# Dense stage of a hybrid decoder layer: places, orders and stores around its two ends

## The reference

```python
h = rms(x);  proj = h @ w_in                       # q | k | v | B | C | xc
a = diff_attention(...);  c = short_conv(...)
x = x + concat(a, c) @ w_out
x = x + peer(rms(x))
# peer: per token and head (8 heads) the 16 best of 128*128 experts, by two lists of 128 keys
act = gelu(einsum("tkd,td->tk", u[experts], h)) * gates
y   = einsum("tk,tkd->td", act, v[experts])        # 128 experts per token
```

## Time and profile before

| | us |
|---|---|
| median of 3 runs | 2944.31 |
| the profiled execution | 2943.42 |
| its span, first to last instruction | 2941.6 |
| TensorE busy | 2884.6 |
| VectorE busy | 2374.1 |
| ScalarE busy | 1054.5 |
| GpSimd busy | 1589.7 |

### The profile page before, as it was taken

One profiled execution on the slowest core, in us unless ns is written; L12 is line 12 of the kernel. 1 busy time (PEld: TensorE's weight loads), 2 busy tenths in 40 slices (PEclk: granted clock), 3 DMA queues, 4 the chain that ended last, 5 costly groups with the idle time before them and its releaser, 6 DMA issues.

```text
span 2941.6 us, 40454 instructions
## 1 busy us (share of the span) xinstructions
PE 2884.6 (98%) x14881; PEld 2557.2 (87%) x14881; DVE 2374.1 (81%) x3078; ACT 1054.5 (36%) x1375; POOL 1589.7 (54%) x1022
## 2 busy tenths in 40 slices
PE   8999999999999999999999999999999999999998
PEld 6888778878899999999999999999997888778777
DVE  6555788755679888988889898899777999889988
ACT  4121433341333333434333343344233333334333
POOL 1000444400115765666656566577867888877852
PEclk9999999999999999999999999999999999999999
DMA  8997887778868999999999899999999999999998
GB/s 296 332 356 271 284 275 262 248 283 312 302 235 311 325 349 316 333 326 341 319 323 340 301 338 330 335 338 368 330 360 395 408 419 416 418 420 420 421 417 359
DMA packets 327440, 995.33 MB, mean 338 GB/s; under 512 B 64565, under 2 KB 181313, under 8 KB 241793
## 3 DMA queue, kind: packets, MB, share of 16 engines
q1 hardware_dynamic: 179056, 515.94, 47.1%
q0 software_dynamic: 110656, 447.10, 42.1%
q10 hardware_dynamic: 37584, 30.43, 3.2%
HBM read 873.67 MB, written 119.67 MB: 338 GB/s over the span
## 4 chain that ended last, share of the span: by engine, by line
PE 69%; DVE 12%; DMA 7%; issue 5%; POOL 5%; ACT 1%; ACTq 0%; DVEq 0%; SPq 0%; POOLq 0%
PE ps L1979 21%; PE ps L1981 21%; PE ps L1980 21%; DMA v_ring<-in_peer_v,experts 4%; DVE x_rows L1829 3%; PE ps L2220 3%; POOL dots L946 3%; POOL v_ring L957 2%; DVE u_row L1820 2%; DMA v_two<-in_peer_v 1%; DVE uT_lo L1788 1%; DVE x_one L1927 1%; DVE uT_lo L1793 1%; DVE v_lo L1878 1%; DMA u_row<-in_peer_u,experts 1%
## 5 line engine op out<-in xcount | busy, mean ns | idle before, releaser
L1979 PE MATMUL ps<-hT_hi,uT_hi 128*128 128x384 f32 x2048 | 698.2, 341 | 8.1 <-DVE uT_lo L1788 4.6
L1981 PE MATMUL ps<-h2T_lo,uT_hi 128*128 128x384 f32 x2048 | 686.0, 335 | 0.0
L1980 PE MATMUL ps<-hT_hi,uT_lo 128*128 128x384 f32 x2048 | 684.9, 334 | 0.0
L938 POOL DMA_INDIRECT grid<-gates,grid_cells x256 | 518.6, 2026 | 105.3 <-issue 78.0
L1979 PE MATMUL ps<-v_hi,a_hi 128*128 128x512 f32 x1024 | 406.8, 397 | 23.5 <-DVE v_lo L1878 22.8
L1980 PE MATMUL ps<-v_hi,a_lo 128*128 128x512 f32 x1024 | 404.7, 395 | 0.0
L1981 PE MATMUL ps<-v_lo,a_hi 128*128 128x512 f32 x1024 | 404.6, 395 | 0.0
L1303 ACT ACTIVATE v_hi<-v_two 128x2048 fp32r<-128x2048 f32 x126 | 241.7, 1919 | 450.9 <-PE ps L1981 385.5
L1979 PEld LDWEIGHTS ps<-hT_hi,uT_hi 128*128 128x128 f32 x2048 | 384.7, 188 | 17.6 <-DVE uT_lo L1788 8.1
L1980 PEld LDWEIGHTS ps<-hT_hi,uT_lo 128*128 128x128 f32 x2048 | 385.0, 188 | 1.9
L1981 PEld LDWEIGHTS ps<-h2T_lo,uT_hi 128*128 128x128 f32 x2048 | 384.4, 188 | 0.0
(11 more groups left out here) (210 smaller groups left out, 4933.8 us busy)
## 6 DMA issues: line engine op xcount, KB each, us to landing
v_two<-in_peer_v SPq DMA_DIRECT2D x63, 2048.0 KB, 11.5
u_tile<-in_peer_u SPq DMA_DIRECT2D x65, 1024.0 KB
u_tile<-uT_all SPq DMA_DIRECT2D x63, 1024.0 KB
grid_rows<-grid SPq DMA_DIRECT2D x32, 1024.0 KB, 15.3
near_rows<-in_peer_u SPq DMA_DIRECT2D x25, 1024.0 KB, 8.7
uT_all<-near_turned SPq DMA_DIRECT2D x100, 256.0 KB, 7.0
w_raw<-in_w_in SPq DMA_DIRECT2D x24, 1024.0 KB, 9.1
wc_raw<-in_w_in SPq DMA_DIRECT2D x48, 512.0 KB, 6.0
```

The costliest lines, as they stand in the source:

```text
L938: pool.indirect_dma_start(out=grid, out_offset=bass.IndirectOffsetOnAxis(ap=grid_cells[:, d, col:col + 1], axis=0), in_=gates[:, 2 + d, co ...
L1979: mm(out, a_hi, b_hi, start=first, stop=False)
L1980: mm(out, a_lo, b_hi, start=False, stop=False)
L1981: return mm(out, a_hi, b_lo, start=False, stop=last)
```

## The change

What it does:

- A new place `v_four` (where a row buffer of u, u_row0, was) takes tile 4, and `v_one` is used a second time, for tile 5. Each is loaded by a DMA of 1 MiB. grid_rows1 moves by 8 KB and the pair buffers a_hi, a_lo change places to make room. v_two[0] is first used for tiles 8 and 9.
- SyncE's order at the front: tile 4, the second group, tile 5, then the third group, tiles 6 and 7, x_one, and on as before. The second group's load no longer waits for the last dots.
- ScalarE splits tile 1 right behind the gelu of the last sweep tile, ahead of the two stores of its products.
- VectorE: `add(126)` comes after tile 1's remainder and the last dot; `weigh_pair(2)` after tile 3's remainder.
- GpSimd: 10 fetches, gathers 2 to 4, the other 6 fetches, gathers 5 to 7.
- `added(tile)` ends one tile sooner: 128 sums over 120 tiles instead of 121.
- The store of x_rows waits until the last remainder is done, and x_end is stored in quarters instead of halves.

```diff
         v_one = at("v_one", 72, [P, D])
+        v_four = at("v_four", 136, [P, D])
...
-        grid_rows = [at(f"grid_rows{i}", kb, [P, GROUP, ROW]) for i, kb in enumerate((176, 112))]
+        grid_rows = [at(f"grid_rows{i}", kb, [P, GROUP, ROW]) for i, kb in enumerate((176, 104))]
...
-        a_hi = [at("a_hi0", 107, [P, 2, GRID], F32R), late_sb("a_hi1", [P, 2, GRID], F32R)]
-        a_lo = [at("a_lo0", 109, [P, 2, GRID], F32R), late_sb("a_lo1", [P, 2, GRID], F32R)]
+        a_hi = [late_sb("a_hi0", [P, 2, GRID], F32R), at("a_hi1", 112, [P, 2, GRID], F32R)]
+        a_lo = [late_sb("a_lo0", [P, 2, GRID], F32R), at("a_lo1", 114, [P, 2, GRID], F32R)]
...
-            return v_one[:, :] if isinstance(h, int) and h == 0 and b < 2 else v_two[b // 2 % 2][:, b % 2, :]
+            if isinstance(h, int) and h == 0 and b in (0, 1, 5):
+                return v_one[:, :]
+            if isinstance(h, int) and h == 0 and b == 4:
+                return v_four[:, :]
+            return v_two[b // 2 % 2][:, b % 2, :]
...
-            for b in range(2):
-                sp.wait_ge(u_used[b], TILES // 2)
-            load_group(1, 1)
-            sp.dma_start(x_one[:, :], x_mid[0]).then_inc(x_in[1], 16)
+            sp.wait_ge(u_used[0], TILES // 2)
+            load_v(0, group=1, into=v_four, landed=v_two_in[0])
             for b in range(2):
                 sp.wait_ge(swept_stored[b], 32 * TILES // 2)
+            load_group(1, 1)
+            sp.wait_ge(v_lo_ready, 2)
+            load_v(1, group=1)
+            sp.wait_ge(u_used[1], TILES // 2)
...
-                    if b % 2 == 1 and not (last and b + GROUP >= TOPK):
+                    if b % 2 == 1 and not (first and b == 1) and not (last and b + GROUP >= TOPK):
                         sp.wait_ge(v_lo_ready, TOPK * h + b + 1)
-                        if first and b == 1:
+                        if first and b == 5:
                             for n in range(2):
                                 sp.wait_ge(v0_used[n], TILES // 2)
                         load_two(group + 1, b // 2 % 2)
+                        if first and b == 3:
+                            sp.dma_start(x_one[:, :], x_mid[0]).then_inc(x_in[1], 16)
...
+            sp.wait_ge(v_lo_ready, TILES)
             sp.dma_start(out_v[0], x_rows[:, 0, :]).then_inc(out_stored, 16)
             sp.wait_ge(v_used, TILES)
             sp.dma_start(out_v[1], x_one[:, :]).then_inc(out_stored, 16)
             for d in range(DENSE):
-                for half in range(2):
-                    cols = slice(half * D // 2, (half + 1) * D // 2)
-                    sp.wait_ge(x_end_ready, TB * d + 2 * half + 2)
+                for m in range(TB):
+                    cols = slice(m * CHUNK, (m + 1) * CHUNK)
+                    sp.wait_ge(x_end_ready, TB * d + m + 1)
                     sp.dma_start(out_v[2 + d][:, cols], x_end[d][:, cols]).then_inc(out_stored, 16)
...
-            for s in range(TOPK):
+            for s in range(10):
                 fetch_product(0, s)
-            for s in range(2, RING):
+            for s in range(2, 5):
+                gather_v(0, s)
+            for s in range(10, TOPK):
+                fetch_product(0, s)
+            for s in range(5, RING):
                 gather_v(0, s)
...
                         .then_inc(swept_kept[b % 2], 1)
+                    if last and b == TOPK - 1:
+                        for n in range(2):
+                            act.wait_ge(swept[n], TILES // 2)
+                        split_v(0, 1, None)
...
-                    for n in sums_of(c):
+                    for n in sums_of(c) if c < TILES - 1 else ():
                         add(n)
...
             def added(tile):
-                return max(0, (tile - FIRST_ADDED) * TILES // (TILES - FIRST_ADDED))
+                return min(TILES, max(0, (tile - FIRST_ADDED) * TILES // (TILES - 1 - FIRST_ADDED)))
...
                 rest_v(1, 1)
                 dot(TILES - 1)
+                add(TILES - 2)
                 rest_v(2, 2)
                 rest_pair(1)
                 add(TILES - 1)
-                weigh_pair(2)
                 for tile in range(3, TILES):
                     pair, b = tile // 2, tile % TOPK
                     rest_v(tile, b)
+                    if tile == 3:
+                        weigh_pair(2)
```

More of the change, by code:

```diff
@@ L729, in v_rows, with load_v @@
                 return v_table[bass.ds(group * GROUP * P, GROUP * P), :].rearrange("(p j) d -> p j d", j=GROUP)
-            def load_v(j):
-                sp.dma_start(v_one[:, :], v_rows(0)[:, j, :]).then_inc(v_one_in, 16)
+            def load_v(j, group=0, into=v_one, landed=v_one_in):
+                sp.dma_start(into[:, :], v_rows(group)[:, j, :]).then_inc(landed, 16)
             def load_two(group, half):
@@ L817, in _ @@
             for d in range(DENSE):
-                for half in range(2):
-                    cols = slice(half * D // 2, (half + 1) * D // 2)
-                    sp.wait_ge(x_end_ready, TB * d + 2 * half + 2)
+                for m in range(TB):
+                    cols = slice(m * CHUNK, (m + 1) * CHUNK)
+                    sp.wait_ge(x_end_ready, TB * d + m + 1)
                     sp.dma_start(out_v[2 + d][:, cols], x_end[d][:, cols]).then_inc(out_stored, 16)
-            sp.wait_ge(out_stored, 16 * (2 + 2 * DENSE))
+            sp.wait_ge(out_stored, 16 * (2 + TB * DENSE))
         @nc_block.gpsimd
@@ L1298, in split_v @@
                     act.wait_ge(v_one_in, 16 * (b + 1))
+                elif isinstance(h, int) and h == 0 and b == 5:
+                    act.wait_ge(v_one_in, 16 * 3)
                 elif b // 2 % 2 == 0:
@@ L1321, in dense @@
                     ahead = not (last and b >= TOPK - 2)
-                    if not (first and b == 0):
-                        if first and b == 1:
-                            for n in range(2):
-                                act.wait_ge(swept[n], TILES // 2)
-                        if not (first and b < 2):
-                            act.wait_ge(v_tile_used, TOPK * h + b - 1)
+                    if not (first and b < 2):
+                        act.wait_ge(v_tile_used, TOPK * h + b - 1)
                         split_v(h, b, None)
```

## The result

The kernel after takes 2951.72 us (median of 17 runs, 2949.7 to 2953.75), the kernel before beside it 2944.36 (17 runs, 2942.4 to 2949.69): ratio 1.0023, 95% interval 1.0017 to 1.0029. It is slower, by 7.4 us where 1.4 were forecast, and 0.4 us above the top of the range (2951.3). The prediction called 0.2% the least that can be told from no change; a ratio of 1.002 lies in the interval, so the loss is at that bound. The profiled execution takes 2951.52 us with a span of 2949.7; before it was 2943.42 and 2941.6, so both measures moved by 8.1.

A forecast was written before the change was run, and what follows sets the result against it. TensorE, busy 98% of the span, bounds the kernel, with DMA setting the dense stage's pace from 2298 to 2880 us; 1.0 + 2.4 - 2.0 = +1.4 on 2943.42 gives 2944.8 us (median 2945.7), range 2936.3 to 2951.3.

The forecast's parts named there:

- The stall at tile 4 goes whole: Dense stage's front: early loads remove TensorE's stall at tile 4; tile 8 could then start 7.4 us sooner.
- The next wait is the first weighing, and holds tile 8: VectorE waits at the first weighing for head 0's fetches; TensorE stands 6.7 us before tile 8.
- The last fetch is issued at 2232.9 and lands 6 us later: GpSimd's last fetch of head 0, behind three gathers and slowed beside busy VectorE, lands at 2238.9.
- Clock loss 1.7 us: TensorE's stand before tile 8 lowers its clock, charged 1.7 us as at tile 4's stall.
- Sums +2.4: Middle of the dense stage: 128 sums over 120 tiles need up to one gather more, about 2.4 us.
- The end -2.0: Kernel's end: earlier last sums and x_end stored in quarters gain 2.0 us.
- A: Rival at the front: fetches land by 2232.4, the first sum isn't held; 2937.3 us as median; chance 0.25.
- DMA's unused 4.4 us: Dense stage's DMA holes at 2220 and 2290, 4.4 us unused, said to pay for most of the unheld front's gain.
- B: Rival at the front: fetches land 3 to 4 us sooner than counted, TensorE stands 3 us; 2941.5; chance 0.15.
- D: Rival at the front: early places do nothing because tile 4 waits for something else; no share of its own.
- C: Rival in the middle: tiles with two sums meet a late gather, 5.6 us per large stand; 2951.3 us; chance 0.14.
- The rule on GpSimd's descriptors: GpSimd's front fetches: 0.94 us beside idle VectorE, 2.04 or 3.04 beside busy, against the skill's inference of no hold-up.

The follow-up runs named there:

- Kernel 8: Kernel after, with three fetches of 128 numbers instead of gathers 2 to 4 between fetches 10 and 11, gathers behind fetch 16: 2949.09 us, ratio 1.0016.
- 3: Kernel before with only the new end: sums over 120 tiles, x_rows' store after the last remainder, quarter stores: 2946.67 us, ratio 1.0007.
- 2: Kernel after with its sums spread over 121 tiles, as before the change: 2950.67 us, ratio 1.0021.
- kernel 1: Kernel after with GpSimd's old order, all 16 fetches of head 0 and then gathers 2 to 7: 2943.79 us, ratio 1.0000.
- 9: On kernel 1, v tiles 8 to 11, 14 and 15 loaded earlier: 2945.28 us, ratio 1.0003.
- 11: On kernel 1, only the store of x_rows moved to the front, behind x_one's load: 2940.72 us, ratio 0.9986.
- 5: Kernel before with gathers 8 to 127 at half a row each: 2930.16 us, ratio 0.9953 to the kernel before.
- 4: Kernel after with the first sum at tile 9 instead of 7: 2943.62 us, ratio 0.9998.
- 6: On kernel 1, gathers 8 to 127 at half a row each: 2931.18 us, ratio 0.9952 to the kernel before.

## Why the forecast was off

The forecast of the profiled execution was 2944.8, and it took 2951.5. Its steps in turn, from tile 0:

- *The stall at tile 4 goes whole*: right. No stand, tile 2 at 11.6 us (forecast 11.7), tile 4 at 22.6.
- *The next wait is the first weighing, and holds tile 8*: right in place and cause. It is wanted at 38.8 us from tile 0, as forecast.
- *The last fetch is issued at 2232.9 and lands 6 us later*: **this is the step that failed**. The issue came 1.2 us later than counted (41.8 against 40.6); the landing took 9.8 us. The 6 us were read off the kernel before's 16 fetches, of which only the first three were issued before the gathers ahead of them had landed (gather 1 lands at 2203.4), while the prediction itself noted that the new order puts three gathers ahead. It had priced them as GpSimd's time only. 1.2 + 3.8 = 5.0, which is all by which the stand was underrated (tile 8 at 56.7 instead of 51.6). Kernel 8 takes the gathers from ahead of the fetches, and 4.0 us of the stand go. Part of the 1.2 us shows at once: the prediction had GpSimd through with gathers 0 and 1 as before, but the first fetch is issued 7.3 us after tile 0, where it was 5.4.
- *Clock loss 1.7 us*: 2.1 (tile 8 to 12 took 24.2 us, 22.1). Tile 12 in all +6.5 instead of +1.0.
- *Sums +2.4*: 0.4 from tile 12 to 127, and 0.7 and 1.2 in the pairs with 3 and 2. Over-priced: it counted the one sum more that is due by then (118 against 117 by tile 118) as a whole gather of the DMA engines' time. The runs show no gather more: the DMA packets from tile 0 to 118 add up to 283.8 to 284.0 MB in before, after, 2 and 3 alike.
- *The end -2.0*: -0.7. x_rows' store was to go at 2927.5, 1.1 us before tile 127; it went with tile 127's start, since that tile's remainder stands behind the two sums of tile 126, which the prediction lists but leaves out here. 4 MiB then have to pass behind tile 127.
- Tile 0 started 2.0 later, no part of the change.

6.7 us in all: 5.4 front, -2.0 sums, 1.3 end, 2.0 start. The mechanism was right and the size of its main term wrong; that the time still came out within 0.4 us of the range owes something to luck, as the overpriced sums hid 2.0 us of the misses.

**The rivals.** A, the first sum isn't held, did not happen in the change, but kernel 1 makes its front: there its gain (forecast 2937.3) failed to arrive, 2943.79. The prediction had let "DMA's unused 4.4 us" pay for the gain, but that time is not consumed by starting sooner. B's front, with a stand of 3 us, is nearly that of kernels 9 and 11 (3.8 and 4.6 us). D is out, since the stand at tile 4 went. C gives 2951.3 and would look like a hit; it isn't, as the stands between tiles 12 and 118 sum to 17.9 us against 16.3. The same time from another mechanism confirms nothing.

**The rule on GpSimd's descriptors.** The fetch at 2213.96 starts beside a tensor_tensor (tile 4's remainder, to 2215.87) and takes 2.73 us, the ones in VectorE's idle time 0.94. The inference in the Trainium skill (SBUF — State Buffer, "Who interferes with whom"), that a tensor_tensor doesn't hold up descriptor generation, does not hold in this trace for indirect DMAs. For GpSimd's plain DMAs it does: in the kernel before, 44 stores of `uT_all` start beside a tensor_tensor of two SBUF inputs (`wc_lo`, 128x1024) and take 0.55 us in the median, as all 176 do. What differs by the code is that an indirect DMA also reads its indices (`cells`, `experts`) in SBUF; that this is the reason is argued, and no run tests it. So the prediction went by its rows rightly, and took for a contradiction what is a difference between two kinds of DMA.

**What is shown and what is argued.** Shown: that GpSimd's order makes the loss (1), that the gathers ahead are 4 us of the hold (8), that half the gathers' bytes take away most of the sums' waits and 14 us (5). Argued: that an early front is given back because the DMA engines, full in the middle, bring the gathers no sooner. In its favour: in eight kernels with whole gathers whose tile 12 comes between 66.8 and 74.4 us, tile 118 lies between 684.0 and 687.1; later fronts (76.4, 80.8) push it to 688.8 and to 691.3 and 692.9. The bytes of before and 1 fit as well. Against a simple account stand 9, where filling the hole did nothing, and 4, whose tiles 12 to 118 took as long as 1's (618.4 us) at 414 GB/s only. The test that would settle it, an early front with light gathers, is missing, as 6 was held. Open are this, and the 12 us of excess left with light gathers.

## What to carry to other kernels

Price a reordering of a DMA queue in both places: the issuing engine's time, and where each transfer stands behind the bytes now ahead of it; a small transfer that something waits for must not be put behind large ones of its own queue. When a stall at the front goes, look for the resource that is full later: behind it, up to 7 us of earlier start were worth nothing here, and 6.5 of later start cost all of it. Move what has to leave the core out of the last microseconds, into a stretch where its data is ready: one store of 1 MiB was worth about 3 us at the end.

## What the runs showed of the hardware

- A fetch of 128 numbers, issued with GpSimd, landed in 3.1 to 8.0 us with small transfers ahead in its queue, and in 9.8 to 15.9 with three 1 MiB gathers ahead (the last six fetches of head 0, in kernel 8 and in the kernel after).
- The stores of x_end landed in 2.2 us on a quiet end, in 4.1 (3.1 to 5.4) behind two stores of 1 MiB.
- The same front code, 0.5 us apart in the issue of one fetch, gave a hold of 0 in one execution and of 5.89 us in another. What the fetch met in between isn't settled; SyncE issued 2 MiB of v tiles at 2231.70 in the one and 2232.13 in the other, with the fetch issued 3.3 and 2.0 us ahead of them. 9 and 11, issued like the second, had 4.87 and 5.62 us.
